# Loading the first two weight slots and x by quarters, with 12 warming matmuls in place of 32

## The chip, the cores and the metric

The kernel runs on one core of a Trainium2 chip. The metric is the device time of one execution in microseconds (us), from the first to the last instruction, with a little around it. TensorE multiplies, ScalarE (ACT) and VectorE (DVE) compute elementwise, GpSimd (POOL) does a few elementwise operations and issues some transfers, and SyncE (SP) issues the rest of the transfers from the chip's memory.

## The reference, cut to what matters

Two blocks follow one another on 256 tokens of width 1024, each of depth 2. The start of the program, which the change touches, is the first feed-forward part of the first block:

```python
def swiglu(h, w_gate, w_up, w_down):
    return (jax.nn.silu(h @ w_gate) * (h @ w_up)) @ w_down
...
    for i in range(DEPTH):
        x = x + 0.5 * swiglu(rmsnorm(x, ffn1_norm[i]), ffn1_w_gate[i], ffn1_w_up[i], ffn1_w_down[i])
```

D_MODEL is 1024 and D_FF is 2816. After it come gated linear attention or latent attention, a cross-attention into 256 memory tokens `mem`, a second swiglu, and then the second block (retention, mLSTM, swiglu, layer norms). All is float32.

## The kernel before, in words

Every weight matrix is cut into slots of 128 x 2048 float32 (1 MB). A slot of a gate or up matrix holds 256 output columns of all 1024 inputs: 8 input tiles (k = 0 to 7) of 256 columns each. `raw`, `whi` and `wlo` are rings of three such slots (RING = 3). Float32 accuracy is made from three fast matmuls: ACT copies a slot to a rounded `whi` (`act_hi`, L233), DVE subtracts to get the rest `wlo` (`dve_lo`, L238), and TensorE computes whi x hi, whi x lo and wlo x hi (`pe_weight`, L242 to L244). The activations are split the same way into `in_hi` (L603) and `in_lo` (L607), 8 tiles of 128 x 256.

SP issues the transfers, all on one queue: params, slot 0, x, slot 1, slot 2, consts (1.6 MB), params2, and then in a loop one slot after another. The transfer of slot 3 waits until slot 0 is fully split (`lo_ready` at 1), that of slot 4 until slot 1 is, and so on (L2338 and L2339). POOL issues the transfer of `mem` (1 MB, L2354) on a queue of its own when all 8 tiles of `in_lo` are written, and then squares and sums it (L354, L357).

TensorE first runs WARM matmuls of zeros (L2431) and then, in `pe_ffn`, in this order: gate of slot 0 (`pe_pair_first`, which follows the tiles of `in_lo` as they come), up of slot 1, the sums of squares of x (L425), gate of slot 2, up of slot 3, and the down matmuls of slot 4, which begin with four clearing matmuls (L303) and wait for `h_lo`, the rest of the first hidden tile.

ACT's order in the same stretch is: hi of slot 0, the 8 tiles `in_hi`, hi of slots 1 and 2, the squares of x (L615), hi of slot 3, a table load, logarithm and exponential of the norm factor (L651, L653), silu (L636), hi of slot 4, `h_hi` (L642). DVE's order is: lo of slot 0, the 8 tiles `in_lo`, lo of slots 1 and 2, the sums of the squares (L623), lo of slot 3, the products around silu (L695, L698, L707), lo of slot 4, `h_lo` (L712). Each engine works in its written order, so a wait holds all that is behind it.

```python
            if normed:
                act_hi(act, c + 2, r3)
            if is_first(f):
                act_first_squares(act)
            act_hi(act, c + 3, r3)
            if normed:
                act_log_exp(act)
                act.wait_ge(fin_sums, f + 1)
```

Of the kernel before, what the change touches and what calls it, by code (L numbers as in the profile page):

```python
# [18 lines left out]
F32 = mybir.dt.float32  # L19
# [3 lines left out]
ACT = mybir.ActivationFunctionType  # L23
# [8 lines left out]
FPAIRS = FF // 256  # L32
SLOT = 2048
RING = 3
WARM = 32
PEEL = 2
HEADS = 4
EPS = 1e-6
# [71 lines left out]
def build(nc, d_slots, d_x, d_mem, d_params, d_params2, d_consts, d_lngb, d_out):  # L110
    with ExitStack() as ctx:
# [76 lines left out]

        fin_hi, fin_lo, fin_step, fin_sq = sem("fin_hi"), sem("fin_lo"), sem("fin_step"), sem("fin_sq")
        first_sq, first_add = sem("first_sq"), sem("first_add")  # L190
        fin_sums, fin_log, fin_factor = sem("fin_sums"), sem("fin_log"), sem("fin_factor")
        consts_loaded, mem_loaded, consts2_loaded = sem("consts_loaded"), sem("mem_loaded"), sem("consts2_loaded")
        mem_sq_done, mem_sums_done, mem_log, mem_factor = sem("mem_sq"), sem("mem_sums"), sem("mem_log"), sem("mem_factor")
# [41 lines left out]
        def dve_lo(dve, c, r=0):  # L235
            j = c % RING
            dve.wait_ge(hi_ready, c + 1 + 3 * r)
            dve.tensor_tensor(wlo[:, j], raw[:, j], whi[:, j].bitcast(F32), ALU.subtract).then_inc(lo_ready, 1)  # L238

        def pe_weight(pe, out, j, o, hi, lo, start, stop, n=P):  # L240

# [149 lines left out]
        def pe_ffn(pe, f, c, r3, parts=None, between=None):  # L391
            fb = f * FPAIRS
            up0_ps, ffn_sums = ffn_banks(f)

            def gate(i, s, i3, out):
                pe.wait_ge(lo_ready, c + s + 1 + 3 * r3 + 3 * i3)
                pe.wait_ge(ffn_silu, fb + i)
                pe_pair(pe, out, (c + s) % RING).then_inc(slot_used, 1)

            def up(i, s, i3, out):  # L400
                pe.wait_ge(lo_ready, c + s + 1 + 3 * r3 + 3 * i3)
                pe.wait_ge(ffn_mul, fb + i)
                pe_pair(pe, out, (c + s) % RING).then_inc(slot_used, 1)

            def down(i, s, i3, hi, lo, first=False):
                pe.wait_ge(lo_ready, c + s + 1 + 3 * r3 + 3 * i3)
                pe.wait_ge(ffn_hl, fb + i + 1)
                if first:
                    pe_clear_acc(pe)
                pe_acc_slot(pe, (c + s) % RING, lambda kk: hi[:, kk], lambda kk: lo[:, kk]).then_inc(slot_used, 1)  # L410

            if is_first(f):
                pe.wait_ge(lo_ready, c + 1)
                pe_pair_first(pe, gate0_ps, c % RING, range(DT), lambda k: pe.wait_ge(fin_lo, k + 1)).then_inc(slot_used, 1)
                up(0, 1, 0, up0_ps)
            else:
                hi_part, lo_part = parts or (lambda k: pe.wait_ge(fin_hi, DT * f + k + 1),
                                             lambda k: pe.wait_ge(fin_lo, DT * f + k + 1))
                pe.wait_ge(lo_ready, c + 2 + 3 * r3)
                pe_pairs_first(pe, (gate0_ps, up0_ps), (c % RING, (c + 1) % RING), hi_part, lo_part)  # L420
            if parts is None:
                pe.wait_ge(consts_loaded, 32)
                pe.wait_ge(fin_sq, f + 1)
                for k in range(2):
                    last = pe.matmul(ffn_sums, ones, sq_ffn[:, k], start=(k == 0), stop=(k == 1), skip_group_check=True)  # L425
                last.then_inc(fin_sums, 1)
            gate(0, 2, 0, gate_ps)
            up(0, 3, 0, up_ps)
            down(0, 4, 0, h_hi, h_lo, True)
            peel = PEEL if is_first(f) else 0  # L430
            for i in range(1, 1 + peel):
                gate(i + 1, 2, i, gate_ps)
                if i == peel:
                    between(pe)
                up(i + 1, 3, i, up_ps)
                down(i, 4, i, h_hi, h_lo)
            with pe.Fori(1 + peel, LASTF) as i:
                gate(i + 1, 2, i, gate_ps)
                up(i + 1, 3, i, up_ps)
                down(i, 4, i, h_hi, h_lo)  # L440
            down(LASTF, FFN_SLOTS - 1, 0, last_hi, last_lo)
# [151 lines left out]
        def wait_down(dve, f, t, h):  # L593
            if t == 1 and h == 1:
                dve.wait_ge(slot_used, FFN_END[f])
            else:
                dve.wait_ge(down_half, 3 * (f - 3) + 2 * t + h + 1)

        def act_ffn_in(act, gain, tiles):

            for k in range(DT):
                tiles(act, k)
                act.activation(in_hi[:, k], x[:, k], ACT.Copy, scale=par(gain, k)).then_inc(fin_hi, 1)  # L603

        def dve_ffn_in(dve, f, gain, k):
            dve.wait_ge(fin_hi, DT * f + k + 1)
# [1720 lines left out]
        @block.sync  # L2327
        def _(sp):
            sp.dma_start(params[:, :], d_params).then_inc(loaded, 16)
            for j in range(RING):  # L2330
                sp.dma_start(raw[:, j], d_slots[j]).then_inc(raw_full[j], 16)
                if j == 0:
                    sp.dma_start(x[:, :, :], d_x.rearrange("(k p) t -> p k t", p=P)).then_inc(loaded, 16)
            sp.dma_start(consts[:, :], d_consts[0]).then_inc(consts_loaded, 16)
            sp.dma_start(params2[:, :], d_params2).then_inc(consts_loaded, 16)
            with sp.Fori(1, SLOTS // RING) as i:
                for j in range(RING):
                    sp.wait_ge(lo_ready, 3 * i + (j - 2))  # L2338
                    sp.dma_start(raw[:, j], d_slots[bass.ds(3 * i + j, 1)].rearrange("a p n -> p (a n)"))\  # L2339
                        .then_inc(raw_full[j], 16)  # L2340
            out = d_out.rearrange("(t p) n -> p t n", p=P)
            y = x[:, :, :].rearrange("p a b -> p (a b)").rearrange("p (t n) -> p t n", t=2)
            last = 4 * 2 * LAYERS
            sp.wait_ge(y_done, last + 2)
            sp.dma_start(out[:, 0], y[:, 0]).then_inc(stored, 16)
            for h in range(2):
                sp.wait_ge(y_done, last + 3 + h)
                sp.dma_start(out[:, 1, 512 * h:512 * h + 512], y[:, 1, 512 * h:512 * h + 512]).then_inc(stored, 16)
            sp.wait_ge(stored, 48)
# [19 lines left out]
        def _(act):  # L2369
# [2 lines left out]
                e.activation(x[:, :, :].rearrange("p a b -> p (a b)"), banks(0, 4, 2048), ACT.Copy).then_inc(x_tok_set, 1)  # L2372
            act.wait_ge(consts_set, 2)
            act.activation(stat[:, 0:1], eps[:, 0:1], ACT.Copy)
            act_hi(act, 0)
            act.wait_ge(loaded, 32)
            for n, (f1, m, f2, out) in enumerate(STAGES):
                act_ffn_in(act, f"ffn1_norm{n}", x_tile(2 * n))
                if n == 0:
                    act_hi(act, 1)  # L2380
                act_ffn(act, 2 * n, f1, 0, True, act_mem_factor if n == 0 else None,
                        then=lambda e: act_mem_hi(e, n))
                act_mem(act, m, n, E_MEM[n])
# [12 lines left out]
        def _(dve):  # L2396
# [1 line left out]
            dve.memset(small[:, :], 0.0)  # L2398
            dve.memset(eps[:, 0:1], EPS).then_inc(consts_set, 1)
            dve.memset(eps[:, 1:2], LN_EPS).then_inc(consts_set, 1)  # L2400
            dve_lo(dve, 0)
            dve.wait_ge(loaded, 32)
            for k in range(DT):
                dve_ffn_in(dve, 0, "ffn1_norm0", k)
            dve_lo(dve, 1)
            for n, (f1, m, f2, out) in enumerate(STAGES):
                dve_ffn(dve, 2 * n, f1, 0, True, lambda e: dve_mem_norm(e, n), lambda e: dve_mem_lo(e, n))
                dve_add(dve, f1 + FFN_SLOTS, 0.5)
# [188 lines left out]
```

## Time and profile before

| what | value |
|---|---|
| median of 3 runs | 2063.55 us (2060.15 to 2065.45) |
| profiled execution, its own time | 2065.46 us |
| profiled execution, span from first to last instruction | 2063.7 us |
| TensorE busy | 2042.7 us, 99% |
| VectorE busy | 1267.6 us, 61% |
| ScalarE busy | 1004.7 us, 49% |
| GpSimd busy | 73.3 us, 4% |
| mean granted TensorE clock | 0.995 |
| moved from and to memory | 362.32 MB, mean 176 GB/s |

The time of an execution is a little above its span. A busy TensorE does not say that the work is at its peak, since matmuls overlap, but it says that hardly any of the span is spent waiting. The change concerns only the first 40 us or so, and what it is worth has to be read there.

### The profile page before, as it was taken

The page shows a single profiled execution, that of the slowest core. Times are in us where ns is not written, and L with a number is a line of the kernel's source. Part 1 is how long each engine was busy: PE and PEld are TensorE (multiplying, and loading weights), DVE is VectorE, ACT ScalarE, POOL GpSimd, SP SyncE. Part 2 cuts the span into 40 slices and gives each one's busy share as a digit, 9 for nine tenths or more (in the row PEclk, how much of TensorE's full clock was granted, in tenths as well). Part 3 has the DMA queues.
Part 4 walks back from the last instruction along what each step waited for, and adds up shares of the span by engine and source line. Part 5 has one row for each costly group of instructions (what it writes and reads, how often), then busy time and mean ns, then how long its engine had stood idle before and what let it go on. Part 6 is the DMA issues. An engine that isn't in the chain of part 4 may idle for free.

```text
span 2063.7 us, 37372 instructions
## 1 busy us (share of the span) xinstructions
PE 2042.7 (99%) x15928; PEld 1956.7 (95%) x15928; DVE 1267.6 (61%) x1163; ACT 1004.7 (49%) x939; POOL 73.3 (4%) x53
## 2 busy tenths in 40 slices
PE   9999999999999999999999999999999999999998
PEld 8999998999999999689999999999998999999997
DVE  6556665655575576656555665675456575676545
ACT  5545645434454457545344663644434554544333
POOL 2000000100010000000000000100000000100000
PEclk9999999999999999999999999999999999999999
DMA  7555452455555544225555444564554434465552
GB/s 299 184 183 183 164 181 105 163 185 190 195 185 191 193 165 167 99 103 213 183 183 184 164 146 162 184 245 157 189 183 164 184 143 151 177 225 184 183 183 102
DMA packets 51218, 362.32 MB, mean 176 GB/s; under 512 B 5680, under 2 KB 6832, under 8 KB 7728
## 3 DMA queue, kind: packets, MB, share of 16 engines
q1 hardware_dynamic: 49856, 353.05, 47.4%
q0 software_dynamic: 1264, 7.80, 1.1%
q8 instruction: 81, 1.33, 0.3%
q14 instruction: 17, 0.14, 0.0%
HBM read 359.78 MB, written 1.05 MB: 175 GB/s over the span
## 4 chain that ended last, share of the span: by engine, by line
PE 94%; DVE 3%; ACT 2%; DMA 1%; issue 1%; DVEq 0%; SPq 0%; ACTq 0%
PE ps L242 23%; PE ps L244 22%; PE ps L243 22%; PE ps L518 3%; PE ps L519 3%; PE ps L517 3%; PE ps L291 2%; PE ps L289 2%; PE ps L290 2%; PE ps L790 1%; PE ps L501 1%; PE ps L495 1%; PE ps L496 1%; DMA raw<-in_slots 1%; ACT whi L233 1%; PE ps L340 1%
## 5 line engine op out<-in xcount | busy, mean ns | idle before, releaser
L238 DVE TENSOR_TENSOR wlo<-raw,whi 128x2048 fp32r<-128x2048 f32 x325 | 755.6, 2327 | 456.5 <-ACT whi L233 455.7
L242 PE MATMUL ps<-in_hi,whi 128*128 128x256 f32 x3596 | 1016.3, 283 | 2.3 <-DVE in_lo L313 2.1
L243 PE MATMUL ps<-in_lo,whi 128*128 128x256 f32 x3596 | 1006.2, 280 | 0.0
L244 PE MATMUL ps<-in_hi,wlo 128*128 128x256 f32 x3596 | 1005.0, 279 | 0.0
L233 ACT ACTIVATE whi<-raw 128x2048 fp32r<-128x2048 f32 x325 | 619.4, 1908 | 194.2 <-PE ps L244 163.5
L242 PEld LDWEIGHTS ps<-in_hi,whi 128*128 128x128 f32 x3596 | 678.3, 189 | 11.0 <-issue 4.9
L243 PEld LDWEIGHTS ps<-in_lo,whi 128*128 128x128 f32 x3596 | 678.3, 189 | 3.2 <-issue 1.4
L244 PEld LDWEIGHTS ps<-in_hi,wlo 128*128 128x128 f32 x3596 | 678.1, 189 | 0.0
L242 PE MATMUL ps<-h_hi,whi 128*128 128x256 f32 x480 | 134.5, 280 | 0.0
L243 PE MATMUL ps<-h_lo,whi 128*128 128x256 f32 x480 | 133.9, 279 | 0.0
L244 PE MATMUL ps<-h_hi,wlo 128*128 128x256 f32 x480 | 133.9, 279 | 0.0
L642 ACT ACTIVATE h_hi<-ws 128x512 fp32r<-128x512 f32 x58 | 36.7, 633 | 195.7 <-PE ps L519 99.4
L712 DVE TENSOR_TENSOR h_lo<-ws,h_hi 128x512 fp32r<-128x512 f32 x58 | 40.9, 706 | 103.1 <-ACT h_hi L642 103.1
L636 ACT ACTIVATE ws<-ws 128x512 f32<-128x512 f32 x44 | 27.8, 632 | 148.1 <-DVE ws L695 148.0
L519 PE MATMUL ps<-whi,h_lo 128*128 128x512 f32 x240 | 94.9, 396 | 0.0
L518 PE MATMUL ps<-wlo,h_hi 128*128 128x512 f32 x240 | 94.9, 396 | 0.0
L517 PE MATMUL ps<-whi,h_hi 128*128 128x512 f32 x240 | 94.9, 395 | 0.0
L289 PE MATMUL ps<-whi,in_hi 128*128 128x256 f32 x320 | 91.1, 285 | 0.0
L242 PEld LDWEIGHTS ps<-h_hi,whi 128*128 128x128 f32 x480 | 90.2, 188 | 0.4
L243 PEld LDWEIGHTS ps<-h_lo,whi 128*128 128x128 f32 x480 | 90.2, 188 | 0.1
L244 PEld LDWEIGHTS ps<-h_hi,wlo 128*128 128x128 f32 x480 | 90.2, 188 | 0.0
L290 PE MATMUL ps<-wlo,in_hi 128*128 128x256 f32 x320 | 89.9, 281 | 0.0
(296 smaller groups left out, 2153.9 us busy)
## 6 DMA issues: line engine op xcount, KB each, us to landing
raw<-in_slots SPq DMA_DIRECT2D x333, 1024.0 KB, 4.8
ws<-in_lngb POOLq DMA_DIRECT2D x4, 1024.0 KB, 5.0
ws<-in_mem_t POOLq DMA_DIRECT2D x2, 1024.0 KB, 10.0
consts<-in_consts SPq DMA_DIRECT2D x1, 1600.0 KB, 14.5
consts<-in_consts POOLq DMA_DIRECT2D x1, 1472.0 KB, 6.7
x<-in_x_t SPq DMA_DIRECT2D x1, 1024.0 KB, 7.7
y<-x SPq DMA_DIRECT2D x1, 512.0 KB, 2.6
y<-x SPq DMA_DIRECT2D x2, 256.0 KB, 2.1
```

The lines of the kernel that those rows point to most:

```text
L233: act.activation(whi[:, j], raw[:, j], ACT.Copy).then_inc(hi_ready, 1)
L238: dve.tensor_tensor(wlo[:, j], raw[:, j], whi[:, j].bitcast(F32), ALU.subtract).then_inc(lo_ready, 1)
L242: pe.matmul(out, whi[:, j, o:o + n], hi, start=start, stop=False, skip_group_check=True)
L243: pe.matmul(out, whi[:, j, o:o + n], lo, start=False, stop=False, skip_group_check=True)
L244: return pe.matmul(out, wlo[:, j, o:o + n], hi, start=False, stop=stop, skip_group_check=True)
L289: pe.matmul(o, a_hi, w_hi, start=(k == 0), stop=False)
L290: pe.matmul(o, a_hi, w_lo, start=False, stop=False)
L291: last = pe.matmul(o, a_lo, w_hi, start=False, stop=(k == DT - 1))
L517: pe.matmul(o, hi[:, kk, a], whi[:, j, w], start=(first and kk == 0), stop=False, skip_group_check=True)
L518: pe.matmul(o, hi[:, kk, a], wlo[:, j, w], start=False, stop=False, skip_group_check=True)
L519: last = pe.matmul(o, lo[:, kk, a], whi[:, j, w], start=False, stop=False, skip_group_check=True)
L712: dve.tensor_tensor(flat(lo), src, flat(hi).bitcast(F32), ALU.subtract).then_inc(ffn_hl, 1)
```

## The change

Slots 0 and 1 and x are cut in quarters (PIECES = 4). A quarter of a slot is 128 x 512 (two input tiles, 256 KB), a quarter of x is two tiles. SP issues quarter by quarter, slot 0 and x in turn, then the quarters of slot 1, then slot 2 and the rest as before. ACT and DVE split quarter by quarter and do the two tiles of x between, and TensorE takes both slots by tiles, waiting for each quarter; for slot 1 that means `pe_pair_first` (with its clearing matmul) in place of `pe_pair`. The zeros matmuls at the start go from 32 to 12.

```diff
-WARM = 32
+WARM = 12
+PIECES = 4
...
+        PIECE = SLOT // PIECES
+
+        def act_piece_hi(act, c, i):
+
+            act.wait_ge(piece_full[c][i], 16)
+            w = slice(i * PIECE, (i + 1) * PIECE)
+            act.activation(whi[:, c, w], raw[:, c, w], ACT.Copy).then_inc(hi_ready if i == PIECES - 1 else piece_hi, 1)
+
+        def dve_piece_lo(dve, c, i):
+            if i == PIECES - 1:
+                dve.wait_ge(hi_ready, c + 1)
+            else:
+                dve.wait_ge(piece_hi, (PIECES - 1) * c + i + 1)
+            w = slice(i * PIECE, (i + 1) * PIECE)
+            dve.tensor_tensor(wlo[:, c, w], raw[:, c, w], whi[:, c, w].bitcast(F32), ALU.subtract)\
+                .then_inc(lo_ready if i == PIECES - 1 else piece_lo, 1)
+
+        def pe_piece(pe, c, k):
+
+            i, part = divmod(k, DT // PIECES)
+            if part == 0:
+                if i == PIECES - 1:
+                    pe.wait_ge(lo_ready, c + 1)
+                else:
+                    pe.wait_ge(piece_lo, (PIECES - 1) * c + i + 1)
...
             if is_first(f):
-                pe.wait_ge(lo_ready, c + 1)
-                pe_pair_first(pe, gate0_ps, c % RING, range(DT), lambda k: pe.wait_ge(fin_lo, k + 1)).then_inc(slot_used, 1)
-                up(0, 1, 0, up0_ps)
+                def ready(k):
+                    pe_piece(pe, 0, k)
+                    pe.wait_ge(fin_lo, k + 1)
+                pe_pair_first(pe, gate0_ps, 0, range(DT), ready).then_inc(slot_used, 1)
+                pe_pair_first(pe, up0_ps, 1, range(DT), lambda k: pe_piece(pe, 1, k)).then_inc(slot_used, 1)
...
-            for j in range(RING):
-                sp.dma_start(raw[:, j], d_slots[j]).then_inc(raw_full[j], 16)
-                if j == 0:
-                    sp.dma_start(x[:, :, :], d_x.rearrange("(k p) t -> p k t", p=P)).then_inc(loaded, 16)
+            for c in range(2):
+                for i in range(PIECES):
+                    w = slice(i * PIECE, (i + 1) * PIECE)
+                    sp.dma_start(raw[:, c, w], d_slots[c][:, w]).then_inc(piece_full[c][i], 16)
+                    if c == 0:
+                        n = DT // PIECES
+                        sp.dma_start(x[:, i * n:(i + 1) * n, :],
+                                     d_x[i * n * P:(i + 1) * n * P].rearrange("(k p) t -> p k t", p=P)).then_inc(x_full[i], 16)
+            sp.dma_start(raw[:, 2], d_slots[2]).then_inc(raw_full[2], 16)
...
-            act_hi(act, 0)
-            act.wait_ge(loaded, 32)
+            act.wait_ge(loaded, 16)
+            for i in range(PIECES):
+                act_piece_hi(act, 0, i)
+                act.wait_ge(x_full[i], 16)
+                for k in range(i * DT // PIECES, (i + 1) * DT // PIECES):
+                    act_ffn_in_tile(act, "ffn1_norm0", k)
+            for i in range(PIECES):
+                act_piece_hi(act, 1, i)
...
-            dve_lo(dve, 0)
-            dve.wait_ge(loaded, 32)
-            for k in range(DT):
-                dve_ffn_in(dve, 0, "ffn1_norm0", k)
-            dve_lo(dve, 1)
+            dve.wait_ge(loaded, 16)
+            for i in range(PIECES):
+                dve_piece_lo(dve, 0, i)
+                dve.wait_ge(x_full[i], 16)
+                for k in range(i * DT // PIECES, (i + 1) * DT // PIECES):
+                    dve_ffn_in(dve, 0, "ffn1_norm0", k)
+            for i in range(PIECES):
+                dve_piece_lo(dve, 1, i)
```

SP's queue of transfers, from its start, before the change (the row of two is slots 1 and 2; the row of width 3200 is consts):

```order
L2329 DMA params<-in_params 128x83
L2331 DMA raw<-in_slots 128x2048
L2333 DMA x<-in_x_t 128x8x256
L2331 DMA raw<-in_slots 128x2048 x2
L2334 DMA consts<-in_consts 128x3200
L2335 DMA params<-in_params 128x146
```

The end of the same stretch after the change, from the third quarter of slot 0 on:

```order
L2368 DMA raw<-in_slots 128x512
L2371 DMA x<-in_x_t 128x2x256
L2368 DMA raw<-in_slots 128x512
L2371 DMA x<-in_x_t 128x2x256
L2368 DMA raw<-in_slots 128x512 x4
L2373 DMA raw<-in_slots 128x2048
L2374 DMA consts<-in_consts 128x3200
L2375 DMA params<-in_params 128x146
```

Slot 2, consts and params2 keep their places behind slots 0 and 1 and x, and 12 transfers of 256 KB stand where three of 1 MB stood.

ACT from its first split on, before the change (L233 is a whole slot, L603 the tiles of x, L615 the squares of x, and the last row is the hi of slot 3):

```order
L233 ACTIVATE whi<-raw 128x2048
L603 ACTIVATE in_hi<-x,params 128x256 x8
L233 ACTIVATE whi<-raw 128x2048 x2
L615 ACTIVATE ws<-x 128x512 x4
L233 ACTIVATE whi<-raw 128x2048
```

After the change, from the third quarter of slot 0 to the hi of slot 3:

```order
L250 ACTIVATE whi<-raw 128x512
L632 ACTIVATE in_hi<-x,params 128x256 x2
L250 ACTIVATE whi<-raw 128x512
L632 ACTIVATE in_hi<-x,params 128x256 x2
L250 ACTIVATE whi<-raw 128x512 x4
L237 ACTIVATE whi<-raw 128x2048
L650 ACTIVATE ws<-x 128x512 x4
L237 ACTIVATE whi<-raw 128x2048
```

Slot 1 is split behind the last tiles of x, as before, and from the hi of slot 2 on the order is what it was; DVE's order changes in the same way.

TensorE's first rows before the change, with what they wait for:

```order
L2431 MATMUL ps<-zeros 128x512 [waits consts_set]
L2431 MATMUL ps<-zeros 128x512 x31
L256 MATMUL ps<-zeros 128x512 [waits lo_ready]
L242 MATMUL ps<-in_hi,whi 128x256 [waits fin_lo]
L243 MATMUL ps<-in_lo,whi 128x256
```

And after it:

```order
L2479 MATMUL ps<-zeros 128x512 [waits consts_set]
L2479 MATMUL ps<-zeros 128x512 x11
L286 MATMUL ps<-zeros 128x512
L272 MATMUL ps<-in_hi,whi 128x256 [waits fin_lo,piece_lo]
L273 MATMUL ps<-in_lo,whi 128x256
```

The first real matmul now waits for a quarter of slot 0 and for the first tile of x, where it waited for the whole slot.

## Rows read from the trace of the kernel before

**Rows 1.** The page's first part: busy time, share, instructions of each engine.
```profile
PE 2042.7 (99%) x15928; PEld 1956.7 (95%) x15928; DVE 1267.6 (61%) x1163; ACT 1004.7 (49%) x939; POOL 73.3 (4%) x53
```

**Rows 2.** Waits of TensorE, 0 to 200 us: total, times, longest.
```profile
PE ps L303 <- DVE h_lo L712: 0.5, 1, 0.5
```

**Rows 3.** The chain that ended last, in order of time, 0 to 100 us.
```profile
1.20 4.95 DMA raw<-in_slots
...
10.59 12.96 DMA raw<-in_slots
23.57 1.92 ACT whi L233
...
33.76 1.53 DVE h_lo L712
...
35.43 1.02 PE ps L303 x4
```

**Rows 4.** Timeline of SP: start, us, transfer issued.
```profile
1.20 0.42 SPq L2331 DMA_DIRECT2D raw<-in_slots  x1
1.67 0.43 SPq L2333 DMA_DIRECT2D x<-in_x_t  x1
```

**Rows 5.** Timeline of the other engines, 0 to 40 us.
```profile
5.98 4.28 PEld L2431 LDWEIGHTS ps<-zeros 128*128 128x128 bf16 x20 [0.28 <-issue]
9.44 3.32 ACT L603 ACTIVATE in_hi<-x,params 128x256 fp32r<-128x256 f32 x8 [1.35 <-DMA x<-in_x_t]
10.33 3.25 DVE L607 SCALAR_TENSOR_TENSOR in_lo<-x,params,in_hi 128x256 fp32r<-128x256 f32 x8
10.86 0.38 PE L242 MATMUL ps<-in_hi,whi 128*128 128x256 f32 x1
13.89 1.05 POOL L2354 DMA_DIRECT2D ws<-in_mem_t  x1 [13.44 <-DVE in_lo L607]
16.27 2.17 ACT L615 ACTIVATE ws<-x 128x512 f32<-128x512 f32 x4
19.01 2.28 DVE L623 TENSOR_TENSOR ws<-ws 128x512 f32<-128x512 f32 x3
22.70 1.03 PE L425 MATMUL ps<-ws,consts 128*128 128x256 f32 x4
27.93 2.03 POOL L354 TENSOR_TENSOR ws<-ws 128x512 f32<-128x512 f32 x2 [13.00 <-DMA ws<-in_mem_t]
```

**Rows 6.** Transfers, 0 to 60 us: issues, KB each, median us to landing.
```profile
x<-in_x_t SPq DMA_DIRECT2D x1, 1024.0 KB, 7.7
ws<-in_mem_t POOLq DMA_DIRECT2D x1, 1024.0 KB, 14.0
```

**Rows 7.** Transfers in 2.5:3, 7:8 and 16:17 us, then queues in 18:21.
```profile
DMA packets 0, 0.00 MB, mean 0 GB/s; under 512 B 0, under 2 KB 0, under 8 KB 0
...
DMA packets 373, 0.38 MB, mean 382 GB/s; under 512 B 0, under 2 KB 373, under 8 KB 373
...
DMA packets 33, 0.42 MB, mean 422 GB/s; under 512 B 0, under 2 KB 0, under 8 KB 0
...
q1 hardware_dynamic: 97, 0.79, 67.3%
q0 software_dynamic: 94, 0.39, 32.5%
```

**Rows 8.** Groups of instructions by line: busy us, mean ns.
```profile
L238 DVE TENSOR_TENSOR wlo<-raw,whi 128x2048 fp32r<-128x2048 f32 x325 | 755.6, 2327 | 456.5 <-ACT whi L233 455.7
...
L623 DVE TENSOR_TENSOR ws<-ws 128x512 f32<-128x512 f32 x3 | 2.1, 689 | 0.2
...
L712 DVE TENSOR_TENSOR h_lo<-ws,h_hi 128x512 fp32r<-128x512 f32 x58 | 40.9, 706 | 103.1 <-ACT h_hi L642 103.1
```

**Rows 9.** TensorE at 329 us, and its 320:340 window with granted clock.
```profile
329.31 5.41 PE L790 MATMUL ps<-ws 128*128 128x256 f32 x16 [2.93 <-ACT ws L1185]
...
320.00:340.00 20.00, 17.07 (x112) 0.91 0.27 105
```

More of the change, by code:

```diff
@@ L190, in build @@
         first_sq, first_add = sem("first_sq"), sem("first_add")
+        piece_full = [[sem(f"piece{c}_{i}") for i in range(PIECES - 1)] + [raw_full[c]] for c in range(2)]
+        x_full = [sem(f"x_full{i}") for i in range(PIECES)]
+        piece_hi, piece_lo = sem("piece_hi"), sem("piece_lo")
         fin_sums, fin_log, fin_factor = sem("fin_sums"), sem("fin_log"), sem("fin_factor")
@@ L597, in wait_down, with act_ffn_in_tile @@
                 dve.wait_ge(down_half, 3 * (f - 3) + 2 * t + h + 1)
+        def act_ffn_in_tile(act, gain, k):
+            act.activation(in_hi[:, k], x[:, k], ACT.Copy, scale=par(gain, k)).then_inc(fin_hi, 1)
         def act_ffn_in(act, gain, tiles):
@@ L602, in act_ffn_in @@
                 tiles(act, k)
-                act.activation(in_hi[:, k], x[:, k], ACT.Copy, scale=par(gain, k)).then_inc(fin_hi, 1)
+                act_ffn_in_tile(act, gain, k)
         def dve_ffn_in(dve, f, gain, k):
@@ L2374, in _ @@
             act.activation(stat[:, 0:1], eps[:, 0:1], ACT.Copy)
-            act_hi(act, 0)
-            act.wait_ge(loaded, 32)
+            act.wait_ge(loaded, 16)
[6 more added lines that the diff above has]
+                act_piece_hi(act, 1, i)
             for n, (f1, m, f2, out) in enumerate(STAGES):
-                act_ffn_in(act, f"ffn1_norm{n}", x_tile(2 * n))
-                if n == 0:
-                    act_hi(act, 1)
+                if n:
+                    act_ffn_in(act, f"ffn1_norm{n}", x_tile(2 * n))
                 act_ffn(act, 2 * n, f1, 0, True, act_mem_factor if n == 0 else None,
```

## The prediction

> **What bounds the kernel now.** I read the page's first part first: TensorE is busy 99% of the span [rows 1]. So a change at the start can only be worth what it takes off the few microseconds before and between TensorE's first matmuls. Its first real matmul starts at 10.86 us [rows 5]. That is the most that could be thought of as idle; the zeros matmuls before it compute nothing.
>
> Next I read the waits of TensorE. After the zeros, in the first 200 us, it has hardly any: 0.5 us before the clearing matmuls of the down step, ended by `h_lo` [rows 2]. That looks like nothing. But it says that the down step starts at 35.43 us because `h_lo` came then, and not because TensorE was late: TensorE was there 0.5 us earlier. So an earlier start of TensorE alone is worth 0.5 us at that place, and the rest becomes a longer wait there, unless `h_lo` also comes earlier.
>
> So the third view is the chain that ended last, in order of time [rows 3]. It shows where `h_lo` comes from: the transfer of slot 3, issued at 10.59 us when slot 0 had been split, takes 12.96 us to land at 23.55. ACT stands before it, because the hi of slot 3 is written ahead of the norm factor and of silu. It starts at 23.57. From there hi, table load, logarithm, exponential, silu, the split of slot 4 and `h_lo` follow one another until `h_lo` begins at 33.76 and the down step at 35.43. From landing to down step it is 35.43 - 23.55 = 11.88 us, and nothing in it depends on when slots 0 and 1 were multiplied.
>
> Why does slot 3 take 13 us? The transfers show it: the queue runs at 422 GB/s in the window 16:17 [rows 7], and slot 3 lies behind x, slots 1 and 2, consts and params2. Its landing is set by the bytes ahead of it, some 7 MB, and not by its issue. From 18 us on `mem` also takes its part: in 18:21 SP's queue q1 moves 0.79 MB and `mem`'s q0 0.39 MB, 0.13 MB per us [rows 7].
>
> **The change, part by part.**
>
> *Slot 0 and x.* The first transfer is issued at 1.20, x at 1.67 [rows 4]; no data moves in 2.5:3 [rows 7], and the slot has landed at 1.20 + 4.95 = 6.15 [rows 3], x at 1.67 + 7.7 = 9.4 [rows 6]. The two together, 2 MB, still land at about 9.4 when interleaved; a pair of quarters comes every 1.4 us, the first near 5. Per pair ACT needs 0.54 us for the 512 columns (2.17 us for four operations of that size [rows 5]) and 2 x 0.415 for two tiles of x (3.32 for 8, [rows 5]), together 1.37. DVE needs about 0.66 (689 ns [rows 8]) and 2 x 0.406 (3.25 for 8), together 1.47, just above the pace of the data. The first pair is through at about 6.4, which is also when 12 zeros matmuls end (of the 32 the last 20 stand from 5.98 on, 0.21 us each [rows 5]). The last tile of `in_lo` is done near 11.2 instead of 13.6, and TensorE ends slot 0 near 11.9 instead of 16.7.
>
> *Slot 1.* Its quarters have all landed by 12 and are split as fast as DVE goes, by about 13.8. TensorE needs 48 matmuls x 0.117 = 5.6 us, as before, and ends near 17.5, where before it ended at 22.70 [rows 5]. The start is therefore 5.2 us ahead.
>
> *Where the lead goes first.* The sums of squares stand next on TensorE. They need the squares (ACT from 16.27 for 2.17 us, behind the hi of slot 2) and their sums (DVE, from 19.01 for 2.28, [rows 5]). Both come behind the split of slot 2, whose bytes land as before, near 14.4 (9.4 plus 2.1 MB at 0.42 MB per us). So the sums are ready at about 20.9, and TensorE waits 3.4 us from 17.5 on. Gate of slot 2 then ends near 27.5. Up of slot 3 needs the lo of slot 3, which ended at 27.8 before (hi until 25.49 [rows 3], then 2.33 [rows 8]): another small wait. Up ends near 34.
>
> *Where the rest goes.* Then the down step waits for `h_lo`, as it does now. Its time is the landing of slot 3 plus 11.88 us. What moves that landing? (a) Bytes of slots ahead of it: the same. (b) `mem`: it is issued when the last `in_lo` is written (13.89 now [rows 5]), then about 2.4 us earlier. So when slot 3 lands q0 has taken 2.4 x 0.13 = 0.31 MB more, which at 0.40 MB per us is 0.8 us. (c) Rows of 2 KB in place of 8 KB for 2 MB: x, with rows of 1 KB, moves at 382 GB/s against 422 for whole slots [rows 7]. Bounds: nothing, or the whole 10% of 5 us, 0.5 us; the rows are nearer to x's than to 8 KB but long enough to lose less, so I take 0.2. (d) SP issues 9 more transfers at 0.43 us each before consts [rows 4], 4 us; the queue is 7 us deep there, so they hide; if it ran dry they would cost up to that. Together slot 3 lands 1.0 us later.
>
> *POOL beside DVE.* `mem` lands at 13.89 + 14.0 = 27.9 and POOL then squares it [rows 5, 6]. `h_lo` took 1.53 us there, where the mean of the 58 is 706 ns [rows 3, 8]: an instruction of DVE waits behind one of POOL. After the change POOL starts near 25.5 and works some 11 us, so it covers more of the chain. Bounds: `h_lo` free of it, -0.8; one more such wait, +0.8. I take +0.2.
>
> *Zeros.* 20 fewer cost nothing: they lay in time in which TensorE had no data. They are covered by nothing else, and what they kept is the clock, below. The clearing matmul that slot 1 gets (0.2 us) lies in the time ahead of the sums.
>
> The sum: down step at 35.43 + 1.0 + 0.2 = 36.6 us, +1.2 us on the span, and behind it the program is as before. The profiled execution would go from 2065.46 to 2066.7. It lies 1.9 us above the median, so against the median: 2063.55 + 1.2 = 2064.7 us.
>
> **The rivals.**
>
> *A. The whole lead is kept: 2058 us.* The start is 5.2 to 5.6 us ahead. For this `h_lo` would have to come as much earlier, that is slot 3 would have to land near 18. For it speaks only that its issue follows the split of slot 0, which gets no later; against it the bytes ahead of it in one queue. Chance 0.06.
>
> *B. The chain holds but is not delayed, or POOL misses it: 2062 us.* TensorE's 0.5 us and the 0.8 us of `h_lo` are then won. The limit is up of slot 3: 27.8 + 5.6 = 33.4, so at most -2. For it speaks that `mem` was issued at 13.89 and yet moves data only from 18 on, so its data may not start earlier at all. Chance 0.25.
>
> *C. TensorE's clock falls (slower side): 2067 us.* In this trace a wait of 2.93 us ahead of 329.31 was followed by a stretch with the clock at half, 1.2 in place of 2.4 GHz: 0.91 over 20 us, which costs 0.09 x 20 = 1.8 us [rows 9]. The change makes a wait of 3.4 us before the sums. The fall would make gate of slot 2 end at 29.3 and up of slot 3 at 35, still ahead of `h_lo`: hidden. It decides from the point at which the gate step loses more than 2.6 us (36.6 - 34.0), or when the fall comes in the down step, after the second wait; then the price is 1.8 on top of 1.2, so +3. Chance 0.12.
>
> *D. Small transfers lose the rate (slower side): 2080 us.* From issue to first data 1.9 us pass (1.20 to about 3.1, [rows 4, 7]). If each of the 9 more transfers showed that gap, slot 3 would land 17 us later and the kernel would take 17 us more; it is slower by over 0.3% from 0.6 us of gap each. Against it: slot and x are issued 0.47 us apart and land 3.2 us apart [rows 3, 4, 6], so the gaps overlap. Chance 0.03.
>
> The Trainium skill speaks for D: "DMA: Bandwidth & Descriptors", section Bandwidth, has the rule to batch transfers to at least 1 MiB for 75% of the peak, and its fit for one transfer has about 2 us fixed. By that rule quarters of 256 KB would be a loss, of the size of D. The trace, in which transfers queue behind one another, doesn't bear it out.
>
> **How the numbers follow.** The forecast has 0.52, A 0.06, B 0.25, C 0.12, D 0.03; 0.02 is left. 0.3%, about what a measurement of this kernel can tell from no change, is 6.2 us, more than A gives. The three runs of before lie 5.3 us apart, so a median may be off by 2 us. Same by that bound: all but D and the edges of A and C, 0.91; faster 0.05, slower 0.04. The range leaves out A and D: from B's limit, 2063.55 - 2 and 1 us of scatter, to C's 2066.6 and 2 us of scatter: 2060.5 to 2068.5.
>
> **What would show it.** TensorE's first real matmul near 6.5 instead of 10.86; a wait of 3 to 4 us before the sums, ended by the DVE sums of the squares; a wait of over 1 us before the down step ended by `h_lo`; slot 3 landing within a microsecond or so of 24.5, `mem` data from about 15.5 on. The prediction is wrong if the down step starts before 34 or after 39, if the hi of slot 3 doesn't wait for its transfer, or if a difference of over 3 us arises behind 40 us, where nothing was changed.

## The result, and the profile after

The changed kernel took 2070.31 us (median of 12 runs, 2065.71 to 2072.79), the kernel before 2065.32 us beside it (12 runs, 2060.15 to 2069.85). The ratio is 1.0023, with a 95% interval from 1.0014 to 1.0032: 5 us slower, clear of zero though below 0.3%. A second set of 11 runs later gave 1.0017 (1.0008 to 1.0026), 3 us. The forecast was 1.2 us slower, 2064.7 us, and a range up to 2068.5. It was worked out from a median of 2063.55 over three runs; the 12 runs of the kernel before gave 2065.32, so 1.8 us of the distance to 2070.31 lie in that starting point.

TensorE's waits in the first 200 us, of the kernel after (total, times, longest), answer to [rows 2]:

```profile
PE ps L457 <- DMA params<-in_params: 3.7, 1, 3.7
PE ps L272 <- DVE in_lo L642: 1.7, 2, 1.5
```

Where 0.7 us of waiting stood before (the 0.5 of [rows 2], and 0.2 before the up matmuls of slot 1) there are 5.4, and the largest wait stands before the sums of squares (L457). The timelines of TensorE, then ACT, DVE, POOL and SP in the same kernel answer to [rows 3 to 5]:

```profile
7.45 0.36 PE L272 MATMUL ps<-in_hi,whi 128*128 128x256 f32 x1 [1.50 <-DVE in_lo L642]
...
19.56 0.27 PE L274 MATMUL ps<-in_hi,wlo 128*128 128x256 f32 x1
23.57 2.07 PE L457 MATMUL ps<-ws,consts 128*128 128x256 f32 x4 [3.73 <-DMA params<-in_params]
...
37.97 0.28 PE L274 MATMUL ps<-in_hi,wlo 128*128 128x256 f32 x1
38.19 1.02 PE L333 MATMUL ps<-zeros 128*128 128x512 bf16 x4
38.86 0.47 PE L272 MATMUL ps<-h_hi,whi 128*128 128x256 f32 x1
...
16.67 1.92 ACT L237 ACTIVATE whi<-raw 128x2048 fp32r<-128x2048 f32 x1 [1.84 <-DMA raw<-in_slots]
26.41 1.91 ACT L237 ACTIVATE whi<-raw 128x2048 fp32r<-128x2048 f32 x1 [5.74 <-DMA raw<-in_slots]
...
20.83 2.28 DVE L658 TENSOR_TENSOR ws<-ws 128x512 f32<-128x512 f32 x3
37.36 0.68 DVE L747 TENSOR_TENSOR h_lo<-ws,h_hi 128x512 fp32r<-128x512 f32 x1
...
12.91 1.05 POOL L2394 DMA_DIRECT2D ws<-in_mem_t  x1 [12.46 <-DVE in_lo L642]
...
8.16 0.51 SPq L2374 DMA_DIRECT2D consts<-in_consts  x1
```

The reader should follow TensorE down: its first real matmul is at 7.45 instead of 10.86, it has done slots 0 and 1 at 19.8 instead of 22.6, and then it loses all of it and more. The sums start at 23.57 (22.70 before), and the clearing matmuls of the down step at 38.19 (35.43 before). That is 2.76 us late. `h_lo` ends at 37.36 + 0.68 = 38.04, and TensorE's last matmul ahead of the step starts at 37.97, matmuls following one another by 0.12: the two limits stand side by side. Slot 3 landed at 26.4 instead of 23.55, and already slot 2, for which ACT did not wait before, made it wait until 16.67.

So close are they that the profile's chain of what ended last no longer passes through slot 3 and `h_lo`. It passes through params2, the sums and TensorE's own matmuls up to the down step:

```profile
8.71 14.81 DMA params<-in_params
23.57 2.07 PE ps L457 x4
...
38.25 0.96 PE ps L333 x4
```

The granted clock in TensorE's windows of the kernel after (us, busy, clock, transfers' share and GB/s):

```profile
20.00:22.00 2.00, 0.00 (x0) 0.94 1.03 361
22.00:24.00 2.00, 0.43 (x1) 0.50 1.03 401
24.00:26.00 2.00, 2.00 (x7) 0.50 1.03 430
26.00:28.00 2.00, 2.00 (x12) 0.50 0.99 414
28.00:30.00 2.00, 2.00 (x16) 0.85 0.74 307
```

The clock went to 1.2 GHz in the wait and came back at about 28.7, so some 5 us of the gate step ran at half speed. The transfers in 3:9 and 9:12, in the first block of the kernel before, in the second of the one after:

```profile
DMA packets 1200, 2.23 MB, mean 371 GB/s; under 512 B 32, under 2 KB 1056, under 8 KB 1056
...
DMA packets 173, 1.29 MB, mean 429 GB/s; under 512 B 16, under 2 KB 16, under 8 KB 16
```

```profile
DMA packets 1380, 1.76 MB, mean 293 GB/s; under 512 B 102, under 2 KB 940, under 8 KB 1380
...
DMA packets 652, 1.03 MB, mean 342 GB/s; under 512 B 62, under 2 KB 247, under 8 KB 651
```

From 3 to 12 us the change moved 2.79 MB where 3.52 MB had been moved: 0.73 MB, or 1.7 us at 0.43 MB per us. The 16 engines that carry the transfers were not idle meanwhile: SP's queue took 95% of them in 3:9 and all of them in 9:12 (99% and all before). They moved fewer bytes in the same busy time.

Behind 38 us the kernel runs as before. I laid ACT's timeline of after beside that of before: the lag is 2.8 us at 36 us and the same up to 860. At the waits near 865, 1240, 1710 and 1860 it changes by up to 1.5 us either way (at the end it is 4.4), where the clock falls and rises at another moment. In the second profiled run of the same kernel the lag is 3.0 at 36, goes up to 5.4 at 1390 and ends at 3.4. So of the 5 us some 3 are seen to belong to the start. The second set agrees: its spans are on average 3.1 us longer than those of the kernel before (2067.2 against 2064.0). That the rest only moves from run to run is not shown.

### The profile page after: what moved, and what is told of

The parts are those of the page before. It is cut to its first block, busy times and chain, and to the rows that moved or that the text cites. A ratio compares the mean times of both kernels' runs of the same rounds, so it can differ in the third digit from the quotient of the medians.

```text
span 2068.0 us, 37362 instructions
## 1 busy us (share of the span) xinstructions
PE 2042.2 (99%) x15909; PEld 1957.6 (95%) x15909; DVE 1268.0 (61%) x1169; ACT 1006.1 (49%) x945; POOL 72.5 (4%) x53
## 3 DMA queue, kind: packets, MB, share of 16 engines
HBM read 359.78 MB, written 1.05 MB: 174 GB/s over the span
## 4 chain that ended last, share of the span: by engine, by line
PE 94%; DVE 3%; ACT 2%; issue 1%; DMA 1%; SPq 0%; DVEq 0%; ACTq 0%
PE ps L272 23%; PE ps L273 22%; PE ps L274 22%; PE ps L550 3%; PE ps L551 3%; PE ps L549 3%; PE ps L321 2%; PE ps L319 2%; PE ps L320 2%; PE ps L825 1%; PE ps L533 1%; PE ps L527 1%; PE ps L528 1%; PE ps L370 1%; DMA params<-in_params 1%
```

## The experiments

Two theories stood at first. **T**: transfers move slower, slot 3 lands late, and the chain behind it sets the down step. **K**: the clock falls in the wait before the sums and TensorE itself is late. The place is measured in each profile by the first matmul with `h_hi`, the step's first real one: 36.10 before, 38.86 after. It comes 0.67 us behind the start of the step's four clearing matmuls, which is the time that the expectations speak of.

| kernel | slot 3's hi starts | sums start | `h_lo` ends | first `h_hi` matmul | ratio to before (95%) |
|---|---|---|---|---|---|
| before | 23.57 | 22.70 | 35.28 | 36.10 | 1 |
| after | 26.41 | 23.57 | 38.04 | 38.86 | 1.0023 (1.0014 to 1.0032) |
| after, again | 26.62 | 23.60 | 38.28 | 39.09 | 1.0017 (1.0008 to 1.0026) |
| after with 32 zeros | 26.50 | 23.48 | 38.15 | 38.97 | 1.0010 (1.0001 to 1.0019) |
| after, kept busy | 26.78 | 23.75 | 38.42 | 39.24 | 1.0012 (1.0003 to 1.0021) |
| after, whole transfers | 21.34 | 24.77 | 34.53 | 37.52 | 0.9994 (0.9985 to 1.0003) |
| the same, 32 zeros | 22.61 | 22.56 | 34.81 | 35.62 | 1.0001 (0.9992 to 1.0010) |
| before with 12 zeros | 22.38 | 24.33 | 34.81 | 37.08 | 1.0001 (0.9992 to 1.0010) |
| after, mem later | 24.38 | 23.23 | 35.20 | 37.65 | 1.0008 (0.9999 to 1.0017) |
| after, quarters by partitions | 30.04 | 26.55 | 42.69 | 43.51 | one run: 2072.46 us, before 2065.89 |
| after, short rows in whole transfers | 22.46 | 24.43 | 34.45 | 37.18 | one run: 2065.97 us, before 2065.89 |
| before, constants and mem later | 18.28 | 22.57 | 31.23 | 35.33 | 0.9996 (0.9987 to 1.0005) |
| after, constants and mem later | 20.48 | 23.16 | 32.66 | 37.61 | 1.0008 (0.9999 to 1.0017) |
| the last, reordered | 19.84 | 26.24 | 34.90 | 36.35 | 1.0005 (0.9996 to 1.0014) |

In the three rows with constants and mem later, the hi of slot 3 starts behind the squares and not at the landing, which came earlier. The intervals are some 2 us wide to either side. They tell the change from before, but hardly the variants from one another; what follows rests on the profiles' times, each from one execution.

**The changed kernel once more.**

> The changed kernel once more beside the others, to have its time on the same chip in the same rounds: ratio 1.0023 again, within 0.001. Theory K and T both leave it as it is.

Measured: 1.0017, and the places of the start within 0.3 us of the first profile (the row "after, again"). The two limits again stand side by side: `h_lo` ends at 38.28, and TensorE's last matmul ahead of the step starts at 38.18.

**32 zeros again.**

```diff
-WARM = 12
+WARM = 32
```

> The changed kernel with 32 zeros matmuls again (the rest of the change stays). Theory T (transfers): the later start comes from slot 3, which lands at 26.4 us where it landed at 23.55, and from the 11.8 us chain behind it; the number of zeros does not touch either, so the down step starts at 38.2 us as in the changed kernel (38.19) and the time stays within 1 us of it. Theory K (clock): the loss is the clock that fell to half at about 21 us after a wait of 3.7 us with little warming before; with 32 zeros TensorE works until 22 us, waits only some 1.5 us before the sums of squares, the clock stays at 2.4 GHz, and the down step starts at about 36, 2 us earlier.

Measured: the down step at 38.29, as T said, and not at 36, as K said. TensorE began slot 0 behind the zeros, at 10.2, the clock stayed at 2.4 GHz, and what the clock gave back ended in waits:

```profile
PE ps L457 <- DMA params<-in_params: 1.5, 1, 1.5
PE ps L272 <- DVE wlo L242: 1.4, 1, 1.4
PE ps L333 <- DVE h_lo L747: 0.8, 1, 0.8
```

The time did not stay as close as T said: 1.0010 is 1.4 to 2.7 us below the change's two ratios, though the intervals overlap (more under what stays open).

**Kept busy before the sums.**

```diff
                 pe_pair_first(pe, up0_ps, 1, range(DT), lambda k: pe_piece(pe, 1, k)).then_inc(slot_used, 1)
+                for _ in range(17):
+                    pe.matmul(gate_ps, zeros[:, 0:P], zeros[:, :], start=True, stop=True, skip_group_check=True)
```

> The changed kernel with 17 more matmuls of zeros (0.216 us each, 3.7 us) between the up matmuls of slot 1 and the sums of squares, so that TensorE has no wait there. Theory K: the clock stays at 2.4 GHz, gate of slot 2 ends near 30 instead of 32, and the time falls by about 2 us. Theory T: up of slot 3 then waits for the lo of slot 3 (31.4) and the down step for h_lo (38.0), so it starts at 38.2 as before and the time moves by less than 0.5 us.

Measured: the clock stayed at 2.4 GHz in every window of the start, TensorE waited 1.4 us for slot 3's lo and 0.8 for `h_lo`, and the step began at 38.57. So at the down step a kept clock is worth nothing as long as `h_lo` comes at 38. In the runs (1.0012) the time is 1 to 2 us below the change's, more than T's half microsecond, and again within overlapping intervals.

**Whole transfers, splits by quarters.**

```diff
-            for c in range(2):
-                for i in range(PIECES):
...
+            for c in range(2):
+                sp.dma_start(raw[:, c], d_slots[c]).then_inc(raw_full[c], 16)
+                if c == 0:
+                    sp.dma_start(x[:, :, :], d_x.rearrange("(k p) t -> p k t", p=P)).then_inc(x_full[0], 16)
...
```

> The changed kernel with the four transfers of before (slot 0, x, slot 1, each whole); the splits and matmuls stay by quarters, 12 zeros stay. Theory T: slot 3 lands near 24 again (a few tenths later than 23.55, since mem is issued about a microsecond earlier), h_lo comes near 36, and most of the loss of 2.8 us at the down step is gone: between 35.4 and 36.5. Theory K: TensorE still has a wait of 3 us or so before the sums, the clock falls, and the down step starts no earlier than 37.5.

Measured: slot 3 landed at 21.3, even before its time in the kernel before, and `h_lo` ended at 34.53. T holds for the landing, but not all of the 5.1 us to the change are the transfers' own: DVE's splits came later here, so `mem` was issued at 15.43 and not at 12.91, and had moved 0.5 MB when slot 3 landed, where it moved all of its 1.05 MB in the change. Yet the step did not start until 36.8, between what T gave (36.5 at the latest) and K (37.5 at the earliest). By then `h_lo` had been ready for 2.3 us, so here TensorE is the limit. It waited 4.0 us before slot 0 and ran it at half clock:

```profile
8.00:10.00 2.00, 0.00 (x0) 0.87 1.08 422
10.00:12.00 2.00, 1.37 (x6) 0.50 1.03 430
12.00:14.00 2.00, 2.00 (x12) 0.50 1.07 445
14.00:16.00 2.00, 2.00 (x11) 0.50 1.03 435
```

**Before with 12 zeros.**

```diff
-WARM = 32
+WARM = 12
```

> The kernel before with 12 zeros matmuls in place of 32 and nothing else. TensorE then has nothing from 6.3 to 10.9 us. Theory K: the clock falls in or soon after that wait, slots 0 and 1 are partly multiplied at 1.2 GHz, up of slot 1 ends about 1.8 us later than 22.7, and since TensorE was only 0.5 us ahead of h_lo at the down step, that starts 1.3 us later: +1.3 us. Theory T: if the clock does not fall there, nothing changes (within 0.5 us).

Measured: TensorE waited 5.8 us, the clock fell, the sums came at 24.33 (22.70 before) and the first `h_hi` matmul 1.0 us late. K as expected (it gave 1.3), though slot 3 landed 1.2 us earlier here than in the kernel before, with `mem` issued 0.85 us later; and in the runs too little to tell (1.0001).

**Whole transfers with 32 zeros.** On the kernel with whole transfers and splits by quarters:

```diff
-WARM = 12
+WARM = 32
```

> The run with whole transfers and splits by quarters, with 32 zeros matmuls instead of 12. There slot 3 landed at 21.3 us and h_lo came at 34.5, yet the down step started only at 36.8, since TensorE waited 4 us from 6.6, its clock fell to half and it was late. If the clock is what held it, then with 32 zeros it stays at 2.4 GHz, up of slot 3 ends near 34.3, and the down step starts between 34.5 and 35, 2 us earlier than with 12 zeros and 0.5 to 1 us before the kernel before; ratio 0.9995 to 1.0000. If it is not the clock, the down step stays at 36.8.

Measured: first `h_hi` matmul at 35.62, 1.9 us earlier than with 12 zeros and 0.5 before the kernel before, as much as TensorE had waited there. This is the price of the fallen clock, and at least that: `h_lo` ended within 0.3 us of its time in the run with 12 zeros, and with 32 TensorE still waited 0.3 us for it.

**mem later.**

```diff
-            pool.wait_ge(fin_lo, DT)
+            pool.wait_ge(lo_ready, 4)
             pool.dma_start(mem, d_mem.rearrange("(k p) t -> p k t", p=P)).then_inc(mem_loaded, 16)
```

> The changed kernel with the transfer of mem issued when slot 3 is split (lo_ready at 4) instead of when x is, so that it cannot share the time of slot 3. Theory M (mem): in the runs so far slot 3 lands the later the earlier mem is issued (21.3 us for an issue at 15.4, 22.4 for 14.7, 23.5 for 13.9, 26.4 to 26.8 for 12.8 to 12.9). Slot 2 lands at 16.65 in the changed kernel; 1.7 MB of constants and 1.05 MB of slot 3 at 0.42 MB per us behind it give 23.2. So slot 3 lands near 23.2, 3.2 earlier, h_lo comes near 35, and the down step is then set by TensorE, with the fallen clock and lo of slot 3, near 36. Theory R (rows or number of transfers alone): mem hardly matters, slot 3 lands after 25.5.

Measured: slot 3 landed at 24.4, 2.0 us earlier than in the change and 1.2 later than expected. So `mem` is a part of the delay, but 0.8 us against before are left though `mem` no longer takes part at all, where in the kernel before it did. The step began near 37.0, 1 us later than expected, held by TensorE: a wait of 3.9 us before the sums, then half clock.

**Number of transfers or length of rows.** Two runs for the transfers alone. One cuts the quarters by partitions, so that rows keep 8 KB; every split then waits for all four:

```diff
-            act.wait_ge(piece_full[c][i], 16)
+            for s in piece_full[c]:
+                act.wait_ge(s, 16)
...
-                    w = slice(i * PIECE, (i + 1) * PIECE)
-                    sp.dma_start(raw[:, c, w], d_slots[c][:, w]).then_inc(piece_full[c][i], 16)
+                    q = slice(i * 32, (i + 1) * 32)
+                    sp.dma_start(raw[q, c], d_slots[c][q]).then_inc(piece_full[c][i], 16)
```

> The changed kernel with the quarters of slots 0 and 1 cut by partitions (32 partitions of 8 KB rows each) and the splits waiting for all four: as many transfers of 256 KB as in the change, but with the long rows of before. If the short rows cost the time, slot 2 lands near 14.5 us (it lands at 16.65 in the changed kernel); if the number of transfers costs it, near 16.6.

The other keeps whole transfers, but lays slots 0 and 1 out in memory as blocks of 128 x 512:

```diff
-                    sp.dma_start(raw[:, c, w], d_slots[c][:, w]).then_inc(piece_full[c][i], 16)
+                sp.dma_start(raw[:, c].rearrange("p (a b) -> p a b", a=PIECES), blocks(c)).then_inc(raw_full[c], 16)
...
```

> The run with whole transfers, but slots 0 and 1 lie in memory as four blocks of 128 x 512, so that each is one transfer of 512 rows of 2 KB: three transfers of slots and one of x as before, with the short rows of the change. If the short rows cost the time, slot 2 lands near 16.6 and ACT waits for it; if the number of transfers costs it, ACT does not wait for slot 2 (its hi starts at 16.24 behind slot 1, as in the run with whole transfers) and slot 3 lands near 21.3 to 22.

The transfers in 3:9, then 9:12, by partitions, and below them those with short rows:

```profile
DMA packets 949, 1.51 MB, mean 252 GB/s; under 512 B 93, under 2 KB 860, under 8 KB 860
...
DMA packets 351, 0.71 MB, mean 238 GB/s; under 512 B 40, under 2 KB 296, under 8 KB 296
```

```profile
DMA packets 1602, 2.18 MB, mean 363 GB/s; under 512 B 31, under 2 KB 1049, under 8 KB 1602
...
DMA packets 499, 1.22 MB, mean 406 GB/s; under 512 B 16, under 2 KB 22, under 8 KB 461
```

Short rows in few transfers keep nearly the rate of before (3.40 MB from 3 to 12 us against 3.52), and ACT did not wait for slot 2. The packets show it too: over these 9 us a packet of 2 KB took 89 ns on average here, and 96 to 107 ns in the change and its variants with the same 12 transfers, while the 1 KB packets of x took 47 to 49 ns in all of them. Long rows in 12 transfers are worst: slot 2 landed at 19.1, outside what either explanation gave, and an 8 KB packet took 522 ns, where it took 317 in the kernel before. So a transfer over 32 partitions has a loss of its own. The second of the two clears the length of rows; the first does not measure the number alone. Each was executed once.

**Constants and mem later**, on the kernel before and on the change: only the columns of consts that the sums need stay ahead of slot 3, slots 3 and 4 go ahead of the other columns and params2, and `mem` is issued as in the run above.

```diff
-            sp.dma_start(consts[:, :], d_consts[0]).then_inc(consts_loaded, 16)
+            sp.dma_start(consts[:, 0:NCOMMON], d_consts[0, :, 0:NCOMMON]).then_inc(consts_first, 16)
+            for j in range(2):
+                sp.wait_ge(lo_ready, 1 + j)
+                sp.dma_start(raw[:, j], d_slots[3 + j]).then_inc(raw_full[j], 16)
+            sp.dma_start(consts[:, NCOMMON:], d_consts[0, :, NCOMMON:]).then_inc(consts_loaded, 16)
...
```

> The kernel before with consts cut in two: 256 columns stay behind slot 2, the rest (1.5 MB) and params2 go behind slot 4, and mem is issued when slot 3 is split. Slot 3 has 1.5 MB less ahead of it and no mem beside it: it lands near 18 to 19 us instead of 23.55 and h_lo is early. TensorE then sets the down step: 34.9 instead of 35.43, -0.5 us. So no more than 1 us faster, which a timing does not tell from the same.

> The changed kernel with the same reordering of consts, params2 and mem. The cost of the 12 transfers stays (slot 2 at 16.6), but slot 3 lands near 19.5 and the chain no longer sets the down step. The sums still come at 23.1 (DVE), TensorE waits 3.3 us before them, and if the clock falls there, gate and up end near 36.5, else near 35: down step at 35 to 36.5 instead of 38.2, and 2 to 3 us less than the changed kernel.

Measured on before: first `h_hi` matmul 0.8 us earlier, without a wait of TensorE. The two runs also set the price of the 12 transfers apart from `mem`, which moved nothing until slot 3 was split: slot 3 landed at 17.1 on before (issued at 10.41, 6.7 us) and at 19.3 on the change (11.61 and 7.7), 2.2 us later. Measured on the change, the plainest reading of K: `h_lo` ended at 32.66, and TensorE came to the step only near 36.9. It waited 3.56 us before the sums, for DVE:

```profile
23.16 1.88 PE L461 MATMUL ps<-ws,consts 128*128 128x256 f32 x4 [3.56 <-DVE ws L662]
```

The clock fell there, in TensorE's windows:

```profile
22.00:24.00 2.00, 0.84 (x3) 0.84 0.99 409
24.00:26.00 2.00, 2.00 (x9) 0.50 0.99 407
26.00:28.00 2.00, 2.00 (x16) 0.81 0.93 279
```

The first `h_hi` matmul came 1.5 us later than before even with slot 3 out of the way. The step near 36.9 is 0.4 us beyond the upper end of what I expected, and the gain on the change 1.25 us and not 2 to 3.

**Reordered.** The last kernel, with the sums behind slot 2's gate matmuls, slot 1 loaded whole and 18 zeros:

```diff
...
+            if parts is None and not is_first(f):
+                sums()
             gate(0, 2, 0, gate_ps)
+            if parts is None and is_first(f):
+                sums()
...
```

> The former with slot 1 as one transfer, 18 zeros matmuls, and the sums of squares moved on TensorE behind the gate of slot 2. TensorE then waits only for the lo of slot 2 (near 20, for less than 1.5 us) instead of for the sums, the clock stays at 2.4 GHz, gate ends near 25.7, up of slot 3 near 32, and the down step starts when h_lo is there, between 32.5 and 34: 1.5 to 3 us before the kernel before (ratio 0.9986 to 0.9993). If the lead of the quarters can't be kept in this way, it starts after 35.

Measured: the waits at the front shrank to 1.0 and 0.3 us, and TensorE reached the down step near 32.7. But now `h_lo` hung on the later sums and ended at 34.90, later than I had worked out; TensorE waited 2.6 us and the clock fell there, so the first `h_hi` matmul came at 36.35, and the ratio is 1.0005. The lead was made and lost again. No variant is shown to beat the kernel before.

## Why the prediction was wrong

**What held.** That an earlier start is not kept, since the down step waits for the chain behind slot 3; that slot 3 would land later and so make the change a small loss; that the wait would come before the sums (3.4 forecast, 3.7 measured, though it was params2 and not DVE that ended it). D's reason held in part, see below. None of the signs of being wrong came up: the step started at 38.2, ahead of 39, the hi of slot 3 waited for its transfer, and no single difference behind 40 us was over 1.5. But one sign that it named did not come: a wait of over 1 us before the down step, where TensorE had none. What is wrong are the sizes at the start.

**The term that was mis-sized: slot 3's landing, +1.0 forecast, +2.8 measured.** The step that failed is "(d) ... so they hide", priced at nothing. The issues did hide, as it says: slot 2 was issued at 7.69 and consts at 8.16, long before their turn. What does not hide is that the split transfers themselves move less. Of the 0.73 MB missing from 3 to 12 us, 0.12 MB, 0.3 us, stand for the short rows, by the run with short rows in whole transfers. "(c) Rows of 2 KB in place of 8 KB" with its 0.2 us was about right. The other 0.61 MB, 1.4 us, come with 12 transfers in place of 3, some 0.16 us for each of the 9 more (an estimate from the totals of these runs). A second effect was in no term. Slot 3 and all that lies ahead of it are 7.0 MB, and with whole transfers and splits by quarters SP's queue had moved just these when slot 3 landed. It had moved 7.56 MB in the kernel before and 7.77 in the change, so a part of slot 4 went ahead of the last of slot 3, 0.2 MB or 0.5 us more than before. With constants and mem later it was 0.65 MB on the change and nothing on before, and the landings lie 2.2 us apart. "Its landing is set by the bytes ahead of it" is therefore only a lower bound.

`mem` had the right size by luck. It was forecast to be issued 2.4 us earlier, to take 0.31 MB more and to cost 0.8 us. It was issued 1.0 us earlier (12.91 against 13.89). Yet by slot 3's landing it had moved all of its 1.05 MB against 0.75, 0.30 MB more, or 0.7 us at 0.41 MB per us: it began 1.0 us earlier (17.2 against 18.2) and took 0.57 MB in 18:21, where it took 0.39 before. Rows, number, rest of slot 4 and `mem` make 0.3 + 1.4 + 0.5 + 0.7 = 2.9, estimates from the bytes moved, for the 2.8 measured.

My argument against D compared only slot 0 and x, which are large; between them nothing shows. D was priced at all of 1.9 us for each transfer or nothing, where a tenth of it or less was the truth. The 1.9 us were themselves read too long: 0.08 MB had moved in 2:2.5 already, ahead of the empty window. The page "DMA: Bandwidth & Descriptors" of the Trainium skill, section Bandwidth, advises batching to 1 MiB or more; by that rule this change loses, and here it did. The same page of the Trainium skill, in its section "Anatomy of one DMA", fits one transfer alone on GpSimd's path with about 2 us fixed. The estimate from these runs, on SP's queue, is a tenth of that or less.

**The mechanism that was called hidden: the clock.** Rival C said that the fall would be hidden because gate and up would still end ahead of `h_lo`. They ended just with it (37.97 + 0.12 against 38.04), because of two things the working had left out, and because the fall itself cost some 2.0 us up to the step (TensorE's way to it without its waits, against the same with 32 zeros: 38.09 against 38.29 - 0.8 - 1.4). The sums waited not only for the squares but for params2, which landed at 23.52, late for the same reason as slot 3; and the squares themselves were late, for slot 2 landed at 16.67 instead of 14.4. With the sums 2.7 us later than I had them (23.57 against 20.9) and the half clock behind, TensorE was itself at the limit. Removing either limit alone gives nothing or half: a kept clock 0.4 us later than the change, the earlier slot 3 (constants and mem later) 1.25 us earlier; without the 12 transfers and with 32 zeros both go, and the first `h_hi` matmul is 3.2 us earlier than in the change. Since a kept clock gave nothing, the 2.8 us of the change are the landing's; the clock stood just behind, hidden as rival C said, but by 0.1 us and not by 1.6.

**POOL beside DVE, +0.2 forecast, -0.1 measured.** `h_lo` itself took 0.68 us in place of 1.53, but lo of slot 3 took 3.08 in place of 2.3. From the start of slot 3's hi to the end of `h_lo` there were 11.63 us against 11.71: they cancel.

**From 2.8 us to 5.** The 2.8 us alone would have given 2063.55 + 2.8 = 2066.4, inside the range. That the time lies outside it comes from the starting point, 1.8 us too low, and from 2.2 us more between the two medians that the start does not explain.

**What stays open.** Why the runs of the change with 32 zeros and with TensorE kept busy (1.0010, 1.0012) lie below those of the change (1.0023, 1.0017) at the same down step. The intervals overlap. In the profiles the differences arise at 337, 865, 1390 and 1710 us, where the clock's falls differ from execution to execution; that they do so by chance is argued, not shown. Over all runs the mean granted clock was 0.9936 in the change and 0.9949 to 0.9950 with 32 zeros, kept busy and before. The one fall at the start, 6.8 us at half speed, accounts for 0.0016 of that, so on average the later falls were not more in the change. What then makes its runs 1 to 3 us slower than those two, at the same down step, is open. How much of the 0.16 us for each transfer is its own and how much comes from taking x and slot 0 in turn was not measured apart; in 10:12, with little of x left, the change still moved 356 GB/s against 421 with short rows in whole transfers. The runs on the length of rows and on partitions were executed once each.

## What to carry to other kernels

Cutting a load to start early pays only if what stands behind the early part also comes early. Here the chain of waits named the later load (slot 3, behind 7 MB) as the limit, and more transfers in the same queue made just that one later. When two limits stand within a few tenths of one another, an experiment that removes one shows nothing; remove both before calling either harmless. And warming matmuls are part of the timing: they cost nothing while TensorE has no data, and taking them out exposes the next wait to the clock.

## What the runs showed of the hardware

- Twelve transfers of 256 KB (slots 0 and 1 and x by quarters) moved 293 and 342 GB/s in 3:9 and 9:12, where three of 1 MB (slot 0, x, slot 1) moved 371 and 429, and three with the slots in 2 KB rows 363 and 406. With the slots' quarters over 32 partitions each it was 252 and 238.
- The loss lay in longer packets and not in gaps: SP's queue took 95% of the 16 engines in 3:9, and 2 KB packets took 96 to 107 ns in place of 89.
- `mem`'s transfer, issued by POOL, moved its first data 4.2 to 4.7 us behind its issue in the profiles, whether the transfer engines were busy meanwhile (13.89 to 18.2 in the kernel before, shares of 0.98 and more) or partly idle (28.92 to 33.3 in the run with mem later, a share of 0.25 in 30:31).
- At the start, waits of TensorE from 2.6 us (reordered) to 6.0 us (quarters by partitions) were each followed or accompanied by 1.2 GHz for some microseconds; waits of 1.5 us (32 zeros) and 2.0 us (quarters by partitions) were not. The length of the wait does not decide alone: one of 2.93 us ahead of 329 us brought the fall in the kernel before (0.91 over 320:340), and one of 2.92 at the same place did not when TensorE was kept busy at the start (1.00).
- Replacing 12 zeros by 32 ahead of whole transfers gave back 1.9 us.
